# A two-layer attention and expert block: router logits and token rows made block by block from x before its norm

## The chip, the cores and the metric

One Trainium2 chip, one core of it. The metric is the device time of one execution in microseconds (us); the figure is the median over runs. TensorE's clock has two levels, 1.2 and 2.4 GHz, and the profile shows the granted share of the higher one for each stretch.

## The reference

256 latent tokens and 256 context tokens of width 1024 go through two layers. Only what comes before and around the router matters here:

```python
x_lat = x_lat + g1 * y_lat                                   # y_lat = merged branches @ w_out
h_lat = rmsnorm(x_lat, norm2_g[l]) * (1.0 + sc2) + sh2
x_lat = x_lat + g2 * grouped_moe(h_lat, ...)                 # the context tokens too, in layer 0

def merge_branches(...):
    g = sigmoid(h @ w_gate + b_gate)
    m = g_a * (o_a @ w_br_mla) + g_b * (o_b @ w_br_na) + g_c * (o_c @ w_br_ft)
    return m @ w_out

def grouped_moe(h, router_w, router_bias, w_g, w_u, w_d):
    scores = sigmoid(h @ router_w)                           # 16 experts in 4 groups of 4
    sel = scores + router_bias
    grp_score = top_k(sel by group, 2)[0].sum(-1)            # the best group, then
    ...                                                      # the 2 best experts in it,
    top_w = top_w / sum(top_w)                               # weights from scores
    hid = silu(h @ w_g[e]) * (h @ w_u[e]) * gate
    return hid @ w_d[e]
```

## The kernel before

**Layout.** All activations are held by feature: `x` is 128 partitions x 8 blocks (kb) x 512 tokens in f32. Large products are made in three passes of 32-bit reduced matmuls (helper `three`, L1436 to L1440): each operand is split into a high part (a cast) and a low part (value minus high part). Weights come in chunks of 1 MB through a ring of five places (`raw`), in halves of 128 x 1024: ScalarE casts the high part (`half_high`, L518), VectorE subtracts to get the low part (`half_low`, L878). TensorE counts used halves in `w_used`, and the two engines run at most four halves ahead.

**Queues.** Each engine has one program, written out by hand, and takes its instructions in order. The waits are on semaphores: `full` and `free` of the 8 PSUM banks, and counters such as `hlo_done`, `mlo_done`, `perm_done`. VectorE's helper `link` waits for the instruction just issued. The function `results` hands out banks ahead of time, in turn or by name.

**Start.** ScalarE squares x block by block, VectorE adds the squares of blocks 0 to 5 (`gather_square`, L894), TensorE sums the result and the last two squares over the partitions (`norm_sum`, L1464, f32, two instructions for each matmul) and spreads the root (`norm_spread`, L1472). The modulation vector is made in four early pieces (`condition`, L1515, and `turn_rows`, L1523), woven between the blocks of the first latent projection (`latent`).

**Merge** (TensorE from L1746, ScalarE L764, VectorE L1162). Four groups of 256 columns. Each has three gate chunks and one branch chunk. The branch chunk has two halves; the first half makes the attention branch for both 128-column blocks (c = 0, 1), the second the other two branches. VectorE waits for the whole chunk, multiplies and adds (L1178 to L1182), ScalarE casts `m_hi` (L784), VectorE makes `m_lo` (L1186). In layer 0 all 512 tokens are carried (nq = 512), in layer 1 only 256.

**Out-projection** (TensorE L1763, VectorE L1190). Four groups (j) of two blocks, two halves each. VectorE adds the result onto x (L1203), ScalarE squares the blocks (L559).

**Second norm and router.** After the last group: `norm_sum`, root (L552), spread over a bank, then for each block VectorE scales x (L926), ScalarE adds the shift into `h_f` (L591), TensorE makes logits (L1795, 16 rows x nq, f32) and, by transposes (L1788), token rows. The sigmoid (L798) is turned again (L1805) to lie by token. VectorE ranks the experts by pairs in small linked instructions (`beaten`, L1226 with the helper `tt`). TensorE counts the tokens ahead of each in its group (L1816 to L1822), VectorE makes the slot of each token and the permutation `perm` (L1306). The token rows in high and low part (L602, L1326) are gathered into 4 units of 128 slots by matmuls (L1836), then gates (`gsl`, L1844) and slots by row (L1851) are made.

**Experts.** Four units and up to three extra units (1 in layer 1), each against four experts. Step i = 0 of the loop is the first expert's up-projection; ahead of step 1 the extra units are gathered (L1924) from the same token rows.

Of the kernel before, what the change touches and what calls it, by code (L numbers as in the profile page):

```python
# [6 lines left out]
F32 = mybir.dt.float32  # L7
F32R = mybir.dt.float32r
# [4 lines left out]
P = 128  # L13
# [45 lines left out]
def build(nc, wts, xin, vecs, rope, dft, biases, out):  # L59
    ctx = ExitStack()  # L60
    with ctx:
# [15 lines left out]
        h_f = nc.alloc_sbuf_tensor_at("h_f", [P, KB, T], F32, offset=h_at)  # L77
        hraw = nc.alloc_sbuf_tensor_at("hraw", [P, T // P, D], F32, offset=h_at + 4 * KB * T)
# [11 lines left out]
        eps = place("eps", [P, 1], F32)  # L90
# [5 lines left out]
        junk = place("junk", [P, 1], F32)  # L96
        smx = place("smx", [P, 4, 8], F32)
# [46 lines left out]
        rt = place("rt", [P, 24, 4, N_EXP], F32, R0)  # L144
        scT = place("scT", [P, T], F32, A0 + 76 * K1)
# [6 lines left out]
        slots = place("slots", [P, 7 * P], F32, A0 + 88 * K1)  # L152
        S0 = A0 + 88 * K1 + 3584
# [3 lines left out]
        gs4 = place("gs4", [P, 8, 4], F32, S0 + 320)  # L157
# [30 lines left out]
        cs_done = sem("cs_done")  # L188
        spread_done = sem("spread_done")
# [93 lines left out]
        for l in range(DEPTH):  # L283
# [24 lines left out]
            s["merge"] = [{"gate": results(6, chunk=True), "br": results(6, chunk=True)} for _ in range(N_MERGE)]  # L308
            s["out"] = [results(2, chunk=True) for _ in range(N_OUT)]
            s["norm2"] = results(2, chunk=True)  # L310
# [5 lines left out]
            s["logit"] = results(1, [0])  # L316
            s["tok"] = [results(1, [1 + i % 6])[0] for i in range(KB)]
            s["score"] = results(1, [7])
            s["rank"] = results(1, [0])
            s["gs"] = results(2 * KB)  # L320
            s["gsl"] = results(1)
            s["row"] = results(1)
# [3 lines left out]
            s["gx"] = [results(1, [6 + i % 2])[0] for i in range(2 * KB)]  # L326
# [58 lines left out]
        def raw_wait(p):  # L385

            return raw_full[ring_slot[p]], 16 * (ring_turn[p] + 1)

# [71 lines left out]
        def _(pool):  # L460
            nc.gpsimd.memset(ident[:], 0.0).then_inc(consts, 1)
            nc.gpsimd.memset(ones[:], 1.0).then_inc(consts, 1)
            nc.gpsimd.memset(eps[:], EPS).then_inc(consts, 1)
# [11 lines left out]
                           allow_small_or_imprecise_dtypes=True).then_inc(tables, 1)  # L475
            nc.gpsimd.iota(first_of[:], pattern=[[P, 4]], base=0, channel_multiplier=0,
# [5 lines left out]
            pool.wait_ge(tables, 6)  # L482
# [22 lines left out]
        def _(act):  # L505
# [30 lines left out]
            def root(res, n, width):  # L536
                b, was = res

                act.wait_ge(full[b], nth(b, was))
                ins = nc.scalar.activation(rinv[:, 0:n], bank[b][:, 0:n], ACT.Sqrt, bias=eps[:], scale=1.0 / width)  # L540
                ins.then_inc(free[b], 1)

                return ins

            def preload(func):

                nc.scalar.activation(junk[:], eps[:], func)

            def norm_root(res, nt):

                act.wait_ge(sum_done, n_norm[0])
                nc.scalar.activation(rs[:, 0:nt // P], bank[res[0][0]][:, 0:nt // P], ACT.Sqrt, bias=eps[:],  # L552
                                     scale=1.0 / D).then_inc(free[res[0][0]], 1)

            def block_square(kb, nt):

                if kb >= 2:
                    act.wait_ge(acc_done, 5 * n_norm[0] + max(kb - 2, 1))
# [17 lines left out]
            def copies(l, which, nt):  # L576
                n0 = (2 * l + which) * KB
                to = h_hi if which == 0 else h_f
                for kb in range(KB):
                    if (l, which) == (0, 0) and kb % 2 == 0:  # L580

                        if kb < 4:
                            half_high(kb // 2)
                        mod_rows(kb // 2)
                        if kb == 4:
                            half_high(2)
                            half_high(3)
                    act.wait_ge(hf_done, n0 + kb + 1)
                    for st in range(nt // S_LAT):
                        c = slice(st * S_LAT, (st + 1) * S_LAT)  # L590
                        ins = nc.scalar.activation(to[:, kb, c], tmp[:, kb % 2, c], ACT.Identity,  # L591
# [1474 lines left out]
```

## Time and profile before

| | us |
|---|---|
| median of 3 runs | 1409.07 |
| lowest, highest | 1408.21, 1409.91 |
| profiled execution | 1407.64 |
| its span | 1405.9 |

| engine | busy us | share | instructions |
|---|---|---|---|
| TensorE, matmuls (PE) | 1295.9 | 92% | 6790 |
| TensorE, weight loads (PEld) | 1012.4 | 72% | 6790 |
| VectorE (DVE) | 886.5 | 63% | 1466 |
| ScalarE (ACT) | 695.8 | 49% | 1064 |
| GpSimd (POOL) | 14.7 | 1% | 28 |

Busy shares are means over stages. A wait is attributed to the engine whose signal came last; matmuls overlap with their neighbours, so the step from one start to the next, not the duration of one, is its price in a dense stretch. The DMA queues move 269 MB, mostly weights, at a mean of 191 GB/s.

### The profile page before, as it was taken

To read this page: it belongs to the slowest core of one execution; us is meant where nothing else is said; L and a number is where in the kernel's file an instruction comes from. 1 tells how busy PE (TensorE), PEld (TensorE's weight loads), DVE (VectorE), ACT (ScalarE), POOL (GpSimd) and SP (SyncE) were. 2 spreads that over 40 slices of the span, in tenths; PEclk is the share of its full clock that TensorE was granted. 3 is DMA by queue.
4 is the path that set the end of the run, shared out by engine and by line. 5 is a ranking of instruction groups with operands and counts; after the bars stand their busy time and mean duration, and the time that the engine had idled before them with its cause. 6 is when DMAs were issued, how large, how long until landed. Compare 5 with 4: busy or idle time off the path is not lost.

```text
span 1405.9 us, 18189 instructions
## 1 busy us (share of the span) xinstructions
PE 1295.9 (92%) x6790; PEld 1012.4 (72%) x6790; DVE 886.5 (63%) x1466; ACT 695.8 (49%) x1064; POOL 14.7 (1%) x28
## 2 busy tenths in 40 slices
PE   5999898989999988799999998899989986999996
PEld 4786555558888865688888886785479974788885
DVE  3655534342444245669999887667645656699985
ACT  3433333342332225358887666444343544588863
POOL 0100000000000000000000000100000000000000
PEclk9999999999999998899999999899999997899997
DMA  7722676642233211059999786332025540699980
GB/s 283 294 91 90 240 300 242 254 164 90 90 102 109 90 60 60 3 221 368 368 367 348 286 315 238 122 110 72 1 73 185 179 140 25 229 370 365 372 309 31
DMA packets 38277, 269.00 MB, mean 191 GB/s; under 512 B 4208, under 2 KB 5360, under 8 KB 5936
## 3 DMA queue, kind: packets, MB, share of 16 engines
q1 hardware_dynamic: 37232, 263.39, 51.2%
q0 software_dynamic: 960, 4.46, 0.8%
q8 instruction: 56, 0.92, 0.3%
q14 instruction: 29, 0.24, 0.0%
HBM read 266.78 MB, written 1.05 MB: 191 GB/s over the span
## 4 chain that ended last, share of the span: by engine, by line
PE 83%; DVE 11%; ACT 3%; issue 2%; DMA 0%; DVEq 0%; SPq 0%; ACTq 0%; PEldq 0%
PE bank L1438 20%; PE bank L1439 20%; PE bank L1440 20%; PE bank L1723 4%; PE bank L1515 3%; DVE lo L878 3%; PE bank L1707 2%; PE bank L1836 2%; PE bank L1682 2%; PE bank L1688 1%; PE bank L1924 1%; ACT w_hi L518 1%; PE bank L1795 1%; PE bank L1523 1%; DVE rt L1226 1%
## 5 line engine op out<-in xcount | busy, mean ns | idle before, releaser
L878 DVE TENSOR_TENSOR lo<-raw,w_hi 128x1024 fp32r<-128x1024 f32 x400 | 485.8, 1233 | 198.6 <-ACT w_hi L518 190.9
L518 ACT CAST w_hi<-raw 128x1024 fp32r<-128x1024 f32 x400 | 416.4, 1051 | 227.7 <-PE bank L1440 221.4
L1438 PE MATMUL bank<-h_hi,w_hi 128*128 128x512 f32 (+1 forms) x512 | 178.9, 349 | 14.0 <-DVE h_lo L938 8.8
L1439 PE MATMUL bank<-h_lo,w_hi 128*128 128x512 f32 (+1 forms) x512 | 177.2, 346 | 0.0
L1440 PE MATMUL bank<-h_hi,lo 128*128 128x512 f32 (+1 forms) x512 | 176.8, 345 | 0.0
L1438 PE MATMUL bank<-w_hi,h_hi 128*128 128x512 f32 (+1 forms) x320 | 127.5, 399 | 0.0
L1439 PE MATMUL bank<-lo,h_hi 128*128 128x512 f32 (+1 forms) x320 | 124.5, 389 | 0.0
L1440 PE MATMUL bank<-w_hi,h_lo 128*128 128x512 f32 (+1 forms) x320 | 123.9, 387 | 0.0
L1438 PEld LDWEIGHTS bank<-h_hi,w_hi 128*128 128x128 f32 x512 | 98.1, 192 | 33.2 <-issue 14.2
L1440 PEld LDWEIGHTS bank<-h_hi,lo 128*128 128x128 f32 x512 | 98.1, 192 | 11.7
L1439 PEld LDWEIGHTS bank<-h_lo,w_hi 128*128 128x128 f32 x512 | 98.2, 192 | 11.2
L722 ACT ACTIVATE prob<-bank,smx 128x512 f32<-128x512 f32 (+1 forms) x72 | 44.3, 616 | 92.7 <-DVE smx L1101 88.7
L1438 PE MATMUL bank<-w_hi,hdT_hi 128*128 128x512 f32 x192 | 76.2, 397 | 3.5 <-DVE hdT_lo L1359 3.5
L1440 PE MATMUL bank<-w_hi,hdT_lo 128*128 128x512 f32 x192 | 76.0, 396 | 0.0
L1439 PE MATMUL bank<-lo,hdT_hi 128*128 128x512 f32 x192 | 75.9, 395 | 0.0
L1440 PEld LDWEIGHTS bank<-w_hi,h_lo 128*128 128x128 f32 x320 | 60.8, 190 | 13.0
L1438 PEld LDWEIGHTS bank<-w_hi,h_hi 128*128 128x128 f32 x320 | 60.7, 190 | 11.8
L1439 PEld LDWEIGHTS bank<-lo,h_hi 128*128 128x128 f32 x320 | 60.8, 190 | 11.1
L784 ACT CAST m_hi<-g 128x512 fp32r<-128x512 f32 (+1 forms) x16 | 8.2, 513 | 114.4 <-DVE g L1182 114.4
L1178 DVE TENSOR_TENSOR g<-g,bank 128x512 f32<-128x512 f32 (+1 forms) x48 | 26.5, 553 | 53.2 <-PE bank L1440 48.5
L1438 PE MATMUL bank<-m_hi,w_hi 128*128 128x512 f32 (+1 forms) x128 | 45.2, 353 | 11.2 <-DVE m_lo L1186 11.2
L1707 PE MATMUL bank<-ident,prob 128*128 128x128 f32 x240 | 35.6, 290 | 20.2 <-DVE prob L1110 20.2
(230 smaller groups left out, 2169.7 us busy)
## 6 DMA issues: line engine op xcount, KB each, us to landing
raw<-weights SPq DMA_DIRECT2D x248, 1024.0 KB, 5.0
x<-tokens SPq DMA_DIRECT2D x2, 1024.0 KB, 6.1
nab<-na_bias POOLq DMA_DIRECT2D x2, 1024.0 KB, 8.3
rp<-rope POOLq DMA_DIRECT2D x2, 512.0 KB, 5.4
ft<-dft POOLq DMA_DIRECT2D x2, 512.0 KB, 6.0
out<-x SPq DMA_DIRECT2D x4, 256.0 KB, 2.2
fd<-dft POOLq DMA_DIRECT2D x2, 128.0 KB, 6.4
vec<-vectors SPq DMA_DIRECT2D x1, 176.0 KB, 2.4
```

Of the source, the lines that this page charges most:

```text
L518: nc.scalar.copy(w_hi[:, g % N_HI, :], raw[:, ring_slot[c], o:o + HALF]).then_inc(hi_done, 1)
L722: nc.scalar.activation(prob[:, i % 2, qb, 0:nk * P], bank[b][:, 0:nk * P], ACT.Exp, bias=smx[:, i % 2, 2 + qb:3 + qb], scale=scale, accum_ ...
L878: nc.vector.tensor_tensor(lo[:, ring_slot[c], o:o + HALF], raw[:, ring_slot[c], o:o + HALF], w_hi[:, g % N_HI, :].bitcast(F32), ALU.subtra ...
L1178: link(nc.vector.tensor_tensor(g3[:, a, c, 0:nq], g3[:, a, c, 0:nq], bank[b][:, 0:nq], ALU.mult))
L1438: nc.tensor.matmul(o, l_hi, r_hi, start=start, stop=False)
L1439: nc.tensor.matmul(o, l_hi, r_lo, start=False, stop=False)
L1440: return nc.tensor.matmul(o, l_lo, r_hi, start=False, stop=stop)
L1515: ins = nc.tensor.matmul(o[32 * j:32 * j + 32, :], cs[:, kb, :], raw[:, ring_slot[p], kb * CW:(kb + 1) * CW], start=(a == 0), stop=(a == 1))
L1682: ins = nc.tensor.matmul(bank[b][:, 0:nk * P], q[:, h, t], k[:, h, k0:k0 + nk * P], start=True, stop=True)
L1707: ins = nc.tensor.transpose(bank[b][:, o:o + P], prob[:, i % 2, qb, kb * P:(kb + 1) * P], ident[:])
L1723: ins = nc.tensor.matmul(bank[b][r:r + 64, 0:S_LAT], vv[:, k0 // P + kb, h * w:(h + 1) * w], probT[:, i % 2, kb, :], start=(kb == 0), stop ...
L1836: ins = nc.tensor.matmul(bank[b][:], h[:, t, kb * P:(kb + 1) * P], perm[:, t, 0:4 * P], start=(t == 0), stop=(t == nt - 1))
```

## The change

It changes what stands between the merge and the experts, and some things around it.

- `h_f` and `hraw` give way to `xc` (x times the norm gain and 1 + scale, without the root) and `xtok` (the same by token). After each out group VectorE writes two blocks of `xc`; TensorE, in the middle of the next group, makes their part of the logits by token (4 or 2 f32 matmuls with `xc` as the weights) and turns them (`token_block`). Blocks 6 and 7 follow after the last group, their logits in one stream with the sum of squares (bank 7).
- The root is applied per token: to the logits on VectorE, to the token rows on ScalarE (`htok_hi`) and VectorE (`htok_lo`), now one instruction per 128 tokens.
- The shift enters the logits as a sum over all features of shift x router weight (`shw`, `shift`), and the gathered rows as one more matmul with four rows (`sh4`, `in_slot`); the four rows are the shift of each of the two streams in high and low part. `in_slot` comes from a matmul of `perm` with a stream indicator.
- The gather adds high and low part in one bank; VectorE then makes `h_lo` as bank minus `h_hi`.
- The ranking compares all pairs in one instruction; the order of work after `perm` is new, and gates and slots by row are made ahead of step 1.
- In the merge the order within the branch chunk on VectorE is new (attention products after its first half; c = 0 before c = 1), and ScalarE and VectorE prepare weight halves at other points.
- At the start the first sum takes only the gathered squares, and `condition(1)` stands ahead of `latent(0)`.

The diff, cut to the parts that the prediction speaks of:

```diff
@@ VectorE, merge
+                    dve.wait_ge(w_used, 2 * s + 1)
+                    gated(0, 0)
+                    gated(0, 1)
+                    half_low(2 * s + 4)
+                    b, was = M["br"][0][2]
+                    dve.wait_ge(full[b], nth(b, was))
+                    gated(1, 0)
+                    gated(2, 0)
+                    merged(0)
+                    chunk_done(s)
+                    gated(1, 1)
+                    gated(2, 1)
+                    merged(1)
+                    merged_low(0)
+                    merged_low(1)
+                    half_low(2 * s + 5)
+                    s += 1
+
+                link(nc.vector.tensor_copy(sh2[:, :, 0:2], mod[:, l, 24:32, :]))
+                nc.vector.tensor_tensor(sh2[:, :, 2:4], mod[:, l, 24:32, :], sh2[:, :, 0:2].bitcast(F32), ALU.subtract)\
+                  .then_inc(sh2_done, 1)
+                for st in range(2):
+                    link(nc.vector.tensor_tensor(
...
+                nc.vector.tensor_reduce(shift[:], shw[:].rearrange("p s k e -> p s e k"), AX, ALU.add).then_inc(shw_done, 1)
@@ TensorE, out-projection
+                def token_block(kb):
+
+                    b, was = L["tok"][kb]
+                    claim((b, was))
+                    if kb == 0:
+                        claim((bs, wass))
+                    pe.wait_ge(xc_done, KB * l + kb + 1)
+                    for t in range(nt):
+                        nc.tensor.matmul(bank[bs][:, 16 + t * N_EXP:16 + (t + 1) * N_EXP], xc[:, kb, t * P:(t + 1) * P],
+                                         vec[:, V_RW + kb * N_EXP:V_RW + (kb + 1) * N_EXP],
+                                         start=(kb == 0 and t == 0), stop=False, skip_group_check=True)
+                    for t in range(nt):
+                        ins = nc.tensor.transpose(bank[b][:, t * P:(t + 1) * P], xc[:, kb, t * P:(t + 1) * P], ident[:])
+                    ins.then_inc(full[b], 1)
...
+                        if a == 0 and j == 0:
+                            b, was = L["shift"]
+                            claim((b, was))
+                            pe.wait_ge(shw_done, l + 1)
...
+                        if a == 0 and j > 0:
+                            token_block(2 * j - 2)
+                            token_block(2 * j - 1)
+                            if j < 3:
+                                shift_rows(j - 1)
@@ VectorE, router
+                def beaten(o, v):
+
+                    vi = v.rearrange("p t (i o) -> p t i o", o=1).to_broadcast([P, nt, 4, 4])
+                    vj = v.rearrange("p t (o j) -> p t o j", o=1).to_broadcast([P, nt, 4, 4])
+                    nc.vector.tensor_tensor(wins[:, 0:nt, :, 0:4], vj, vi, ALU.is_gt)
+                    tt(wins[:, 0:nt, :, 4:8], vj, vi, ALU.is_equal)
+                    tt(wins[:, 0:nt, :, 4:8], wins[:, 0:nt, :, 4:8],
+                       lower_of[:].rearrange("p (o i) j -> p o i j", o=1).to_broadcast([P, nt, 4, 4]), ALU.mult)
+                    total(o, wins[:, 0:nt])
@@ TensorE, gather
+                for kb in range(6):
+                    gathered_high(kb)
+                for kb in range(3):
+                    gathered_low(kb)
+                gathered_high(6)
+                gathered_low(3)
+                gathered_high(7)
+                for kb in range(4, KB):
+                    gathered_low(kb)
@@ TensorE, start
-                pe.wait_ge(acc_done, 5 * n + 5)
-                for i, part in enumerate((rinv, sq[:, 0, :], sq[:, 1, :])):
+                pe.wait_ge(acc_done, acc_from(n + 1))
+                parts = (rinv,) if n == 0 else (rinv, sq[:, 0, :], sq[:, 1, :])
...
                 if l == 0:
+                    condition(1)
                     latent(0)
-                    condition(1)
+                    turn_rows(1)
                     latent(1)
-                    turn_rows(1)
                     condition(2)
```

## Rows read from the trace of the kernel before

**Rows 1.** The page: chain that ended last, shares by engine.

```profile
PE 83%; DVE 11%; ACT 3%; issue 2%; DMA 0%; DVEq 0%; SPq 0%; ACTq 0%; PEldq 0%
```

**Rows 2.** Windows by stage. Columns: window, length, busy (x) of five engines, clock, DMA share, GB/s.

```profile
497.60:537.60 40.00, 39.95 (x162) 32.09 (x163) 16.05 (x24) 12.55 (x16) 0.00 (x0) 0.94 0.23 79
...
537.60:593.50 55.90, 43.79 (x196) 29.78 (x195) 36.38 (x111) 25.35 (x49) 0.88 (x1) 0.79 0.06 19
...
1157.60:1192.20 34.60, 22.88 (x104) 16.05 (x102) 25.41 (x93) 17.55 (x41) 0.88 (x1) 0.75 0.09 31
```

**Rows 3.** Timeline of the start. Columns: start, length, engine, line, operation, count, [idle before].

```profile
12.15 1.84 PE L1464 MATMUL bank<-ones,rinv 128*128 128x1 f32 x8 [12.15 <-DVE rinv L894]
...
17.33 3.64 PE L1515 MATMUL bank<-raw,cs 128*32 128x256 f32 x32
...
26.53 0.80 PE L1438 MATMUL bank<-h_hi,w_hi 128*128 128x512 f32 x1 [3.70 <-DVE h_lo L938]
...
31.64 1.93 PE L1515 MATMUL bank<-raw,cs 128*32 128x256 f32 x32
...
40.68 0.50 PE L1438 MATMUL bank<-h_hi,w_hi 128*128 128x512 f32 x1 [1.49 <-DVE h_lo L938]
```

**Rows 4.** Timeline of TensorE behind the last merge group of layer 0.

```profile
497.65 0.80 PE L1438 MATMUL bank<-m_hi,w_hi 128*128 128x512 f32 x1 [5.45 <-DVE m_lo L1186]
```

**Rows 5.** Waits of TensorE from 1100 to 1160: total, times, longest.

```profile
PE bank L1438 <- DVE m_lo L1186: 5.8, 1, 5.8
```

**Rows 6.** Windows of TensorE alone. Columns: window, length, busy (x), clock, DMA share, GB/s.

```profile
500.00:502.00 2.00, 2.00 (x6) 0.50 0.00 0
...
504.00:506.00 2.00, 2.00 (x10) 1.00 0.45 78
...
589.50:593.50 4.00, 4.00 (x38) 1.00 0.00 0
...
598.60:613.00 14.40, 13.64 (x68) 1.00 0.32 127
...
1137.00:1140.00 3.00, 3.00 (x15) 0.50 0.03 5
...
1144.00:1157.00 13.00, 13.00 (x113) 1.00 0.54 191
...
1197.50:1208.00 10.50, 8.30 (x37) 0.71 0.43 172
...
1208.00:1212.00 4.00, 4.00 (x11) 0.50 0.00 0
```

**Rows 7.** Groups of VectorE by form: busy us, mean ns, idle before.

```profile
L878 DVE TENSOR_TENSOR lo<-raw,w_hi 128x1024 fp32r<-128x1024 f32 x400 | 485.8, 1233 | 198.6 <-ACT w_hi L518 190.9 <-PE bank L1472 3.4
...
L1178 DVE TENSOR_TENSOR g<-g,bank 128x512 f32<-128x512 f32 x24 | 16.5, 686 | 37.7 <-PE bank L1440 35.4
...
L1110 DVE TENSOR_SCALAR prob<-prob,smx 128x256 f32<-128x256 f32 x24 | 8.5, 353 | 0.8
```

**Rows 8.** Timeline behind the out-projection of layer 0.

```profile
537.63 0.95 PE L1464 MATMUL bank<-ones,rinv 128*128 128x1 f32 x8
...
539.52 3.35 PE L1464 MATMUL bank<-ones,sq 128*128 128x1 f32 x16 [0.94 <-ACT sq L559]
...
557.79 1.09 PE L1788 MATMUL bank<-ident,h_f 128*128 128x128 f32 x8
...
559.27 0.22 DVE L1230 COPY rt<-bank 128x64 f32<-128x64 f32 x1 [5.73 <-PE bank L1805]
...
572.03 10.25 PE L1836 MATMUL bank<-perm,htok_hi 128*128 128x512 f32 x32 [5.80 <-DVE perm L1306]
```

**Rows 9.** Timeline of layer 1: an out group, and the scores.

```profile
1140.85 17.29 SPq L435 DMA_DIRECT2D raw<-weights  x4
...
1143.14 0.87 DVE L1203 SCALAR_TENSOR_TENSOR x<-bank,mod,x 128x256 f32<-128x256 f32 x2
...
1170.50 0.19 DVE L1230 COPY rt<-bank 128x32 f32<-128x32 f32 x1 [3.33 <-PE bank L1805]
```

More of the change, by code:

```diff
@@ L156, in build @@
         gsl = place("gsl", [P, 7, 4], F32, S0 + 192)
-        gs4 = place("gs4", [P, 8, 4], F32, S0 + 320)
+        over = place("over", [P, 4, 3], F32, S0 + 320)
+        ahead = place("ahead", [P, 4], F32, S0 + 384)
+        past = place("past", [P, 4], F32, S0 + 416)
+        over4 = place("over4", [P, 4, 4, 3], F32, A0 + 82 * K1)
         gx9 = place("gx9", [P, 3, 3], F32, S0 + 448)
@@ L804, in _ @@
                     act.wait_ge(full[b], nth(b, was))
-                    nc.scalar.copy(h_hi[:, kb, :], bank[b][:]).then_inc(free[b], 1)
-                b, was = L["row"][0]
-                act.wait_ge(full[b], nth(b, was))
-                nc.scalar.copy(sbr[:, 0:nq], bank[b][:, 0:nq]).then_inc(free[b], 1)
+                    nc.scalar.copy(h_hi[:, kb, :], bank[b][:]).then_inc(gshi_done, 1)
                 n_it, n_ext = L["n_it"], L["n_ext"]
@@ L1209, in _ @@
+                    if j == 0:
+                        b, was = L["shift"]
+                        dve.wait_ge(full[b], nth(b, was))
+                        nc.vector.tensor_copy(shift[:], bank[b][:, 0:2 * N_EXP].rearrange("p (s e) -> p s e", e=N_EXP))\
+                          .then_inc(free[b], 1)
+                    s += 1
                 dve.sem_inc(x_done, 1)
-                low(s + 1)
-                norm(l, 1, nq)
-                nt = nq // P
+                nt, ns = nq // P, nq // S_LAT
@@ L1312, in _ @@
                   .then_inc(g4_done, 1)
+                gathered_low(5)
+                half_low(2 * s + 3)
                 for t in range(nt):
@@ L1464, in norm_sum @@
                         ins = nc.tensor.matmul(bank[b][:, t:t + 1], part[:, t * P:(t + 1) * P], ones[:, 0:1],
-                                               start=(i == 0 and t == 0), stop=(i == 2 and t == nt // P - 1))
+                                               start=(i == 0 and t == 0),
+                                               stop=(part is parts[-1] and t == nt // P - 1))
                 ins.then_inc(sum_done, 1)
@@ L1845, in _, with gather @@
                                                start=(t == 0), stop=(t == nt - 1))
-                ins.then_inc(full[b], 1)
-                b, was = L["row"][0]
-                claim((b, was))
-                pe.wait_ge(diag_done, l + 1)
-                for t in range(nt):
-                    ins = nc.tensor.matmul(bank[b][:, t * P:(t + 1) * P], ones[:], diag[:, t, :], start=True, stop=True)
-                ins.then_inc(full[b], 1)
+                    ins.then_inc(full[b], 1)
+                def gather(res, h, kb, c0, c1, start):
+                    b, was = res
+                    for t in range(nt):
+                        pe.wait_ge(htok_done if h is htok_hi else htlo_done, t0 + t + 1)
+                        nc.tensor.matmul(bank[b][:, 0:c1 - c0], h[:, t, kb * P:(kb + 1) * P], perm[:, t, c0:c1],
+                                         start=(start and t == 0), stop=False)
@@ new lines, in shifted, with gathered_high @@
+                def shifted(res, kb, c0, c1):
+                    b, was = res
+                    bi, wasi = L["ind"][c0 // 512]
+                    pe.wait_ge(free[bi], wasi + 1)
+                    for bh, wash in L["sh4"]:
+                        pe.wait_ge(free[bh], wash + 1)
+                    nc.tensor.matmul(bank[b][:, 0:c1 - c0], sh4[:, kb * P:(kb + 1) * P], in_slot[:, c0:c1],
+                                     start=False, stop=True).then_inc(full[b], 1)
+                def gathered_high(kb):
+                    claim(L["gs"][kb])
+                    gather(L["gs"][kb], htok_hi, kb, 0, 512, True)
```

512 lines of the change are left out of this document (292 added, 220 removed).

## The prediction, made before the change was run

> **What bounds the kernel now.** First the chain that ended last: TensorE has 83% of it and VectorE 11% [rows 1]. So time that leaves TensorE's own stream is gained, time added to it is lost, and beyond that only the stretches where TensorE waits for VectorE count. The windows by stage show where those are [rows 2]. In the out-projection of layer 0 TensorE is busy 39.95 of 40.0 us. Between the projection's end (537.6) and the first expert matmul (593.5) it is busy 43.8 of 55.9 us at a mean clock of 0.79, and the same stage of layer 1 has 22.9 of 34.6 us. VectorE works 36.4 us of that first stage, mostly in tiny linked instructions. Three more gaps are in the code the change touches: the first matmuls of the program, 3.70 and 1.49 us inside the first latent projection [rows 3], and the wait for m_lo after the last merge group, 5.45 us in layer 0 [rows 4] and 5.8 us in layer 1 [rows 5]. Each gap costs more than itself. After the 5.45 us the granted clock is 0.50, 1.2 GHz (6 matmuls in 2 us where 9 to 10 run at 1.00, the 2.4 GHz level: 0.43 us a step and, over long stretches, 0.233) [rows 6].
>
> I write T for the end of the last merge group and E for the end of the out-projection; the sum is made on the profiled execution.
>
> **Start.** The sum of squares goes from 24 instructions to 8, as VectorE adds two more squares first. Now it begins at 12.15 with 8 in 1.84, and the condition matmuls start at 17.33 [rows 3]. After: two adds of 0.69 [rows 7] bring the begin to 13.45, and 8 instructions end at 15.3, so 2.0 us earlier. Condition(1), 1.93 us [rows 3], moves from behind latent(0) into the 3.70 us wait: 1.9. Its rows are then turned earlier, so latent(2) no longer waits 1.49. Latent(0) ran its 12 matmuls at 0.43 us a step where 0.23 is the full-clock step, and with less idle time ahead of it should run fast: 2.0. Sum -7.4; bounds 0 (if the weight chunks land no earlier) and -8.
>
> **End of the merge.** The products of block c=0 are multiplied as soon as its banks are full, 2.8 us before T in layer 0. VectorE's chain then is: two products (0.69 each [rows 7]) and two adds to T+0.1, the same for c=1 to T+3.0, the two m_lo to T+4.4. TensorE has 30 matmuls, 7.0 us, of other work behind T before it wants block 6, so the 5.45 us wait goes, and with it the slow stretch of 4.5 us behind it, worth 2.3. But a new wait appears: after the first half of out group 0 TensorE needs the shift logits, and VectorE reaches them only behind a half_low (1.23 [rows 7]) and six small instructions (about 1.4): T+7.0, TensorE is there at T+5.6. Costs 1.4. Queued behind that wait is the whole rest of the projection. Layer 0: -5.45 - 2.3 + 1.4 = -6.3. In layer 1 a half is 2.8 us (24 steps of 0.115 [rows 6]) and VectorE's chain hardly shorter: products and adds 0.42 to 0.45 each (0.44 for 256 columns out of a bank [rows 9]), end of m_lo at T+4.0, half_low to T+5.25, shift at T+6.7, TensorE waiting from T+2.8. So 5.8 becomes 3.9, and the slow clock behind it (3 us at 0.50 [rows 6], worth 1.5) stays half of the time: -2.6.
>
> **Out-projection, which TensorE bounds.** It takes in six token blocks, two shift rows and the shift logits. A logit matmul in f32 is two instructions bound by the weight load, like the sum over squares: 8 in 0.95, so 0.119 [rows 8]. A turn is one of 0.128 (8 in 1.09 with its end) [rows 8]. Layer 0: 4 x 2 x 0.119 + 4 x 0.128 = 1.46 a block, six are 8.8. Eight turns of the shift in f32 at 0.24 are 1.9 (bounds 1.0 and 2.0), the logits 0.25. Sum +10.9. Layer 1 has two token tiles: six at 0.73 are 4.4, with 2.15 that is 6.5. There TensorE also waits: the x update starts 2.3 us after a group's end (group end 1140.85, 1143.14 [rows 9]), two of 0.44, then the scaled copy 0.35 [rows 7]: T'+3.6, while TensorE is through the next half at T'+2.8. Three times 0.8: +2.4. Sum +8.9. In layer 0 the same chain ends 5.2 us after the group, inside the next half of 5.6.
>
> **From E to the first expert matmul.** Layer 0 now: 8 and 16 sum instructions, the latter at 0.21 (slow clock); scores on VectorE at 559.27 = E+21.6; gather at 572.03 = E+34.4 [rows 8]; 64 matmuls in 17.5; then 28 + 8 instructions for gates and rows, 4.0 at full clock [rows 6]; expert at E+55.9. After, at the slow clock for this piece, since the same quiet work lowers it today: squares at E+1.75, 16 sums to E+5.2, 16 logit instructions to E+8.6; root, table load (1.3) and two token copies of 0.6 on ScalarE, sigmoid done at E+11.9. VectorE to the group mask: 9 linked instructions of 0.18 to 0.28, E+14.2. Counting matmuls, 16 at 0.21, with four VectorE instructions under them: E+17.7. Nine small instructions E+19.5, four perm of 0.62 to E+22.1, indicator products to E+23.9. The gather has 64 + 8 matmuls at 0.233, 16.8, plus 0.8 while the clock recovers: E+41.5. Gates and rows (4.0) are not gone, they stand in step 1 on TensorE now. So 41.5 against 55.9 - 4.0: -10.4. The token rows' low part (4 x 1.3) is done at E+27.3, before TensorE wants it at E+30. Layer 1 the same way: sums and logits to E+3.3, sigmoid E+6.1, mask E+8.2, counts E+10.1 (8 at 0.22), first perm E+12.5, indicator E+13.8, gather 40 x 0.233 = 9.3 + 2.4 slow: E+25.5. Today the scores start at 1170.50 [rows 9] = E+12.9, and the expert at E+34.6 [rows 2] of which 1.5 is gates and rows: 33.1. Gain -7.6.
>
> **The gather of the extra units, in step 1.** It now uses one bank per block in place of two. Layer 0: 14.4 us [rows 6] become 72 x 0.17 = 12.3 plus 0.3: -1.8. Layer 1: 10.5 us of which 2.2 idle, and 4 us at 0.50 behind it [rows 6]. After, two banks in turn, each 0.6 (TensorE) + 0.35 + 0.4, is 0.75 a block, 6; if the clock still falls 8.8. I take 7: -3.5.
>
> **Sum:** -7.4 - 6.3 - 2.6 + 10.9 + 8.9 - 10.4 - 7.6 - 1.8 - 3.5 = -19.8. The profiled execution takes 1407.64 us, 1.74 of it outside its span, and lies 1.43 below the median of the runs shown. So 1407.64 - 19.8 + 1.43 = 1389.3. The router's own rewrite is nearly even (10.9 + 8.9 against 10.4 + 7.6): its work leaves a stage where TensorE is partly idle for one where it is not. The gain is the start, the merge and step 1.
>
> **The rivals.**
> (A) Slower: the clock falls inside the out-projection. Token blocks and shift rows are up to 3.9 us of narrow matmuls between dense halves. Each fall would double that piece (about +3 in layer 0, +1.9 in layer 1) and run 4.5 us of the next half at 0.50 (+2.3, +1.6): six of them are 26 us, giving 1415. It decides from four falls of six (+17.6), where the kernel is about even. For it: the 8 narrow sum instructions at 537.63 with 1 us idle behind them are followed by 0.21 steps [rows 8]. Against it: 4.0 us of narrow work at 589.5 keep 1.00 [rows 6]. The Trainium skill (TensorE: Matmul & The Clock Gate, "A second HAM failure mode: psum-queue depth-cycling") tells of short idle moments between matmul groups that move the clock to and fro; by that rule this case would happen, and the 4.0 us row does not agree. Chance 0.08.
> (B) The start stays bound by the arrival of weights and by the modulation chain, and keeps only 2.0 of 7.4; VectorE, with shift, scaled copies and gather parts in its queue, adds 3 more: 1389.3 + 5.4 + 3 = 1398. For it: the matmuls are only one of three things the start needs, and each of the four modulation rounds passes through ScalarE and VectorE. Against it: latent(0) starts behind the very chain (sum, condition(0), spread) that gets shorter. Chance 0.22.
> (C) Quiet pieces behind E run at full clock: 48 + 16 instructions at 0.12 in place of 0.21 in layer 0 is -4.5, rank in layer 1 -0.9, and step 1 of layer 1 stays fast, -3: 1381. Layer 1 shows full clock behind E today, layer 0 doesn't. Chance 0.15.
> (D) Nothing measurable: the ranking chain doesn't shorten, for each paired instruction waits for its result just the same. My count has about 22 linked steps where there are 53; were it 40, 18 x 0.2 x 2 = 7 us come back: 1396, still faster; with B's 9 on top it is 1405, and that is within 0.2% of now (about what a measurement of this kernel can tell from no change). Chance of the two together 0.05.
> The forecast itself, 1384 to 1395, has 0.50. A to D and the forecast make 1.
>
> **Range and chances.** From (C) with 2 us to spare, 1379, to (B) with 3, 1401; outside are (A) and (D). Faster by over 0.2%: forecast, (B) and (C), 0.87; within: (D), 0.05; slower: (A), 0.08.
>
> **What would show it.** Right: no wait on m_lo at the merge's end; a wait of TensorE for VectorE's shift of 1 to 2 us in layer 0 and 3 to 4 in layer 1; the out-projection of layer 0 10 to 12 us longer at clock 1.00; first perm near E+20 and E+12.5; the first feature projection ending about 7 us earlier. Wrong: a clock of 0.5 between out groups, TensorE waiting for xc in layer 0, or a gather bound by VectorE's or ScalarE's copies out of the banks.

## The result, and the profile after

The changed kernel takes 1399.98 us (median, 1399.35 to 1400.46) where the kernel before takes 1408.71 (1408.21 to 1409.91) on the same chip: 0.9936 of it, 95% interval 0.9919 to 0.9954. Timed again beside the later experiments it was 1398.82, a ratio of 0.9928 (0.9913 to 0.9942). So it is faster, by 9 to 10 us; the forecast was 19.8. The two profiled spans are 1405.9 and 1397.9, 8.0 apart. Executions of one kernel differ with the granted clock (the kernel before on another chip: 1408 us at a mean clock of 0.958 to 0.960, 1412 to 1413 at 0.954 to 0.957), so each time below stands with its ratio to the kernel before on the same chip and the 95% interval of that ratio.

First the windows by stage of the changed kernel, cut at the events of the table below (columns as in [rows 2]): start, latents to their first square sums, attention (two), merge of layer 0, its out-projection, its end to the first expert matmul, steps 0 and 1 up to the second feature projection of step 1, experts, layer 1 up to its merge, and then the same stages of layer 1 (whose out-projection is cut here 0.5 us ahead of its first matmul, which starts at 1117.91).

```profile
0.00:24.37 24.37, 8.70 (x83) 5.42 (x83) 10.60 (x25) 11.64 (x20) 2.49 (x18) 1.00 0.94 376
24.37:59.50 35.13, 34.62 (x209) 27.02 (x210) 21.25 (x44) 15.92 (x27) 5.28 (x5) 1.00 0.79 316
...
300.15:478.20 178.05, 178.05 (x769) 146.03 (x770) 67.37 (x77) 51.54 (x63) 0.00 (x0) 0.99 0.25 89
478.20:534.83 56.63, 55.26 (x284) 45.13 (x282) 25.07 (x49) 19.48 (x26) 0.00 (x0) 1.00 0.22 75
534.83:577.52 42.69, 35.51 (x145) 25.85 (x143) 24.47 (x64) 15.90 (x24) 0.90 (x1) 0.76 0.07 25
577.52:602.90 25.38, 25.38 (x134) 20.85 (x133) 11.30 (x21) 8.91 (x14) 0.00 (x0) 1.00 0.23 84
...
1117.40:1154.71 37.31, 31.44 (x249) 29.56 (x247) 19.14 (x40) 15.68 (x26) 0.00 (x0) 0.95 0.32 114
1154.71:1182.25 27.54, 20.22 (x78) 13.16 (x76) 17.42 (x52) 12.63 (x22) 0.90 (x1) 0.75 0.11 38
1182.25:1199.77 17.52, 16.94 (x80) 14.20 (x79) 9.95 (x22) 7.19 (x14) 0.00 (x0) 0.80 0.33 121
```

The stages in both traces, each cut at the start of its first matmul, and what the prediction had for each (its steps regrouped to the cuts, us):

| stage | before | after | difference | forecast |
|---|---|---|---|---|
| start, to the first square sums of the latents | 67.34 | 59.46 | -7.9 | -7.4 |
| attention and merge, layer 0 | 417.71 | 418.73 | +1.0 | 0 |
| out-projection, layer 0, with the wait at its head | 52.58 | 56.64 | +4.1 | +4.6 |
| its end to the first expert matmul | 55.68 | 42.69 | -13.0 | -14.4 |
| steps 0 and 1 with the extra units' gather | 19.45 | 25.33 | +5.9 | +2.2 |
| other experts, layer 0 | 269.04 | 270.18 | +1.1 | 0 |
| layer 1 up to the end of its merge | 245.48 | 244.88 | -0.6 | 0 |
| out-projection, layer 1, with its waits | 30.34 | 36.80 | +6.5 | +6.3 |
| its end to the first expert matmul | 34.61 | 27.54 | -7.1 | -9.1 |
| steps 0 and 1, layer 1 | 15.03 | 17.52 | +2.5 | -2.0 |
| the rest | 198.64 | 198.13 | -0.5 | 0 |

The miss is 11.8 us, and 11.6 of it stand in the four rows behind the two projections, where the gathers are. Each of the other rows is within 1.1 us.

The waits of TensorE in the changed kernel's two out-projections (478 to 540 us, then 1117 to 1160; total, times, longest). The m_lo of [rows 4, 5] is gone; the shift logits have taken its place.

```profile
PE bank L1915 <- DVE shift L1266: 1.4, 1, 1.4
...
PE bank L1915 <- DVE shift L1266: 3.1, 1, 3.1
PE bank L1880 <- DVE xc L1289: 2.4, 3, 0.8
```

And the tail behind the projection of layer 0, where [rows 8] stood (timeline of TensorE; the last line is VectorE's):

```profile
534.83 0.95 PE L1930 MATMUL bank<-ones,rinv 128*128 128x1 f32 x8
536.62 2.85 PE L1930 MATMUL bank<-ones,sq 128*128 128x1 f32 x16 [0.84 <-ACT sq L591]
539.34 3.57 PE L1935 MATMUL bank<-vec,xc 128*128 128x16 f32 x16
...
548.16 0.58 PE L1951 MATMUL bank<-rt,before 128*128 128x16 f32 x2 [3.46 <-DVE rt L1355]
...
553.73 1.28 DVE L1385 TENSOR_SCALAR perm<-slots,slot 128x896 fp32r<-128x896 f32 x2
```

The first of the four perm instructions starts at E+18.9 (forecast E+19.5) and the last ends at E+21.4 (22.1). The first gather matmul starts at E+23.1 (23.9), in layer 1 at E+13.1 (13.8). So routing got ready a little earlier than forecast, and yet the first expert started 1.4 and 2.0 us later than forecast: the time went into the gathers, 19.6 us in place of 17.6 and 14.4 in place of 11.7.

### The profile page after: what moved, and what is told of

Its sections match the earlier page's. It is cut to its first block, busy times and chain, and to the rows that moved or that the text cites. A ratio compares the mean times of both kernels' runs of the same rounds, so it can differ in the third digit from the quotient of the medians.

```text
span 1397.9 us, 18387 instructions
## 1 busy us (share of the span) xinstructions
PE 1306.0 (93%) x6908; PEld 1024.3 (73%) x6908; DVE 877.4 (63%) x1426; ACT 693.1 (50%) x1038; POOL 15.0 (1%) x30
## 3 DMA queue, kind: packets, MB, share of 16 engines
HBM read 266.78 MB, written 1.05 MB: 192 GB/s over the span
## 4 chain that ended last, share of the span: by engine, by line
PE 87%; DVE 8%; ACT 2%; issue 2%; DMA 0%; DVEq 0%; SPq 0%; PEldq 0%; ACTq 0%
PE bank L1539 21%; PE bank L1541 20%; PE bank L1540 20%; PE bank L1826 4%; PE bank L1977 3%; PE bank L1618 3%; PE bank L1810 2%; PE bank L1785 2%; DVE lo L929 1%; PE bank L1791 1%; PE bank L1626 1%; PE bank L2066 1%; PE bank L2067 1%; DVE prob L1162 1%; PE bank L1987 1%
## 5 line engine op out<-in xcount | busy, mean ns | idle before, releaser
L1541 PEld LDWEIGHTS bank<-h_hi,lo 128*128 128x128 f32 x512 | 98.0, 191 | 11.8
L1540 PEld LDWEIGHTS bank<-h_lo,w_hi 128*128 128x128 f32 x512 | 98.2, 192 | 11.3
L1539 PE MATMUL bank<-w_hi,hx_hi 128*128 128x512 f32 x128 | 51.9, 406 | 0.0
L1618 PE MATMUL bank<-raw,cs 128*32 128x256 f32 x768 | 48.0, 392 | 3.0 <-PE bank L1826 3.0
L1541 PE MATMUL bank<-w_hi,hx_lo 128*128 128x512 f32 x128 | 50.7, 396 | 0.0
```

The source lines that it names most:

```text
L1539: nc.tensor.matmul(o, l_hi, r_hi, start=start, stop=False)
L1540: nc.tensor.matmul(o, l_hi, r_lo, start=False, stop=False)
L1541: return nc.tensor.matmul(o, l_lo, r_hi, start=False, stop=stop)
L1618: ins = nc.tensor.matmul(o[32 * j:32 * j + 32, :], cs[:, kb, :], raw[:, ring_slot[p], kb * CW:(kb + 1) * CW], start=(a == 0), stop=(a == 1))
```

## Experiments: the 4-row shift product

In the gather one line is new: `shifted`, which adds the shift of a token's stream to every slot by a product with four rows. A low block with it (four products, the shift product, and the start of the next block), then a block of step 1, in the changed kernel (timeline of TensorE):

```profile
564.83 1.19 PE L1977 MATMUL bank<-perm,htok_lo 128*128 128x512 f32 x4
565.95 0.50 PE L1987 MATMUL bank<-in_slot,sh 4*128 4x512 f32 x1
566.38 0.73 PE L1977 MATMUL bank<-perm,htok_lo 128*128 128x512 f32 x2
...
587.88 0.86 PE L1977 MATMUL bank<-perm,htok_lo 128*128 128x384 f32 x4
588.67 0.44 PE L1987 MATMUL bank<-in_slot,sh 4*128 4x384 f32 x1
589.04 0.98 PE L1977 MATMUL bank<-perm,htok_hi 128*128 128x384 f32 x4
```

From 564.83 to 566.38 are 1.55 us for five steps, where five of 0.233 are 1.17. And the weight load in this place waits, for nothing that the profile can name (timeline of the weight loads):

```profile
564.40 0.18 PEld L1987 LDWEIGHTS bank<-in_slot,sh 4*128 4x128 f32 x1 [0.35 <-issue]
564.83 0.30 PEld L1977 LDWEIGHTS bank<-perm,htok_lo 128*128 128x128 f32 x2 [0.25 <-issue]
```

Theory S: going from 128 rows to 4 and back keeps the loads from running under the matmul before. Rivals: the product costs its columns and the time is elsewhere (W); the three semaphore waits ahead of it cost the time (Q).

**no_shift_product.** The matmul of `shifted` is taken out.

```diff
-                    nc.tensor.matmul(bank[b][:, 0:c1 - c0], sh4[:, kb * P:(kb + 1) * P], in_slot[:, c0:c1],
-                                     start=False, stop=True).then_inc(full[b], 1)
```

> The changed kernel without the 32 products of sh4 and in_slot that add the shift to the gathered rows (the shift is left out of the experts' input). Theory S, the 4-row products are what was mis-sized: in the changed kernel's trace a low block with one takes 1.55 us and four plain steps are 0.93, so 0.62 x 8 in layer 0 and 0.62 x 8 in layer 1; in step 1 it is 1.97 against 1.56, 0.41 x 8, and some 0.35 x 8. Sum 16: about 1384 us. Rival W, each costs its columns as the prediction had it (0.233 and 0.17, narrower in layer 1), and the missing time lies in the clock or in copies out of the banks: 5.6, about 1394 us.

Measured: 1384.84 us, 0.9808 (0.978 to 0.9837), 15 to 18 less than the changed kernel: theory S, not W. (It leaves the shift out of the experts' input, so it only serves to time the rest.)

**waits_once.** The three `wait_ge` only `if kb == 0`.

> The changed kernel with the three semaphore waits ahead of each 4-row product (ind bank, sh4 bank twice) kept only ahead of the first block, where they are not yet met. Rival Q, the waits in TensorE's queue delay the product: up to 0.39 x 16 + 0.2 x 16 = 9 less, about 1391 us. Theory S, the load of 4 rows is what doesn't overlap: no change, 1400 us.

Measured: 1397.86 us, 0.9919 (0.9888 to 0.9949), and the gather's stretches (from the first gather matmul to the first matmul behind step 1's gather) are 45.6 and 32.0 us, where the changed kernel beside the later runs has 45.5 and 31.9. Q falls.

**shift_twice.** The matmul stands twice, the first with `stop=False`.

> The changed kernel with each 4-row product issued twice in a row into the same bank (the shift is added twice). If every 4-row product pays for its own load (0.18 + 0.23 and more): 32 x 0.4 to 0.5, about 1415 us. If only the change from 128 rows to 4 and back costs, the second costs its columns: 5.6 more, about 1406 us.

Measured: 1414.73 us, 1.0015 (0.9994 to 1.0036), which agrees with the first number. But the ten executions run from 1407.2 to 1417.0 us, four of them below 1411 at a mean clock of 0.962 to 0.964 and six above 1413 at 0.956 to 0.958, so the total can't decide between the two. The trace, of an execution of 1409.28 us, can (timeline of TensorE):

```profile
565.19 0.49 PE L1987 MATMUL bank<-in_slot,sh 4*128 4x512 f32 x1
565.53 0.39 PE L1989 MATMUL bank<-in_slot,sh 4*128 4x512 f32 x1
565.85 1.19 PE L1977 MATMUL bank<-perm,htok_lo 128*128 128x512 f32 x4
566.97 0.49 PE L1987 MATMUL bank<-in_slot,sh 4*128 4x512 f32 x1
```

A low block's period goes from 1.55 to 1.78 us (+0.23), one of step 1 from 1.97 to 2.15 (+0.18): the second product costs its columns. The stretches grow by 4.2 and 4.1 us. So the change of shape is paid once for each visit. The span is 10.4 us above that of the changed kernel; some 2 us of it are not located.

**rows_128.** `sh4` and `in_slot` get 128 rows, 124 of them zero; `wide_of` stands in for `of_stream`.

```diff
-        sh4 = place("sh4", [4, D], F32R, A0 + 74 * K1)
+        sh4 = place("sh4", [P, D], F32R, A0 + 74 * K1)
+        wide_of = place("wide_of", [P, 2, P], F32R, A0 + 80 * K1)
...
-        in_slot = place("in_slot", [4, 7 * P], F32R, A0 + 88 * K1)
+        in_slot = place("in_slot", [P, 7 * P], F32R, A0 + 88 * K1)
```

> The changed kernel with sh4 and in_slot of 128 rows, 124 of them zeros (one more ScalarE instruction and three VectorE ones in the out-projection), so that the shift product has the shape of the others. Theory S: a step as any other, so 16 - 5.6 = 10 us less than the changed kernel, about 1390 us, and no idle weight load ahead of the line. Rival: it is not the row count but the end of the accumulation or the waits: 1400 us.

Measured: 1388.17 us, 0.9839 (0.9811 to 0.9866), 11 to 13 us less than the changed kernel, with nothing left out. Spans 1386.6 against 1397.2, 10.6 apart. Its timeline of TensorE:

```profile
562.67 1.07 PE L1988 MATMUL bank<-perm,htok_lo 128*128 128x512 f32 x4
563.58 0.39 PE L1998 MATMUL bank<-in_slot,sh 128*128 128x512 f32 x1
563.80 1.07 PE L1988 MATMUL bank<-perm,htok_lo 128*128 128x512 f32 x4
```

A block is 1.13 us, the stretches are 38.8 and 27.3 us: 11.3 less, while no_shift_product has 37.8 and 26.6. Two products of the same content, with 4 rows or with 128, differ by 0.42 us a block.

**rows_64 and rows_32.** rows_128, but the product reads `sh4[0:64, ...]` and `in_slot[0:64, ...]` (or `0:32`).

> rows_128 with the shift product reading only rows 0 to 63 of the padded tiles (the writes stay those of rows_128). If the load waits whenever the number of rows changes between neighbours: a low block of 1.55 us as with 4 rows, gather's stretches 45.2 and 31.6 us, some 1399 us. If only a few rows are the trouble: 1.13 us a block, 1388 us as rows_128.

> The same with rows 0 to 31. Change of row count: as with 4 rows, 1399 us. Few rows only: between rows_64 and the 4-row kernel. If the padded writes and not the shape of the product were what helped in rows_128, both would be at 1388 us with blocks of 1.13 us.

Measured: 1397.66 us, 0.9926 (0.9899 to 0.9953), and 1399.42 us, 0.9935 (0.9915 to 0.9955). Stretches 45.2 and 32.0, 45.5 and 31.9 us, as with 4 rows. With 64 rows:

```profile
562.74 0.50 PE L1998 MATMUL bank<-in_slot,sh 64*128 64x512 f32 x1
563.16 1.18 PE L1988 MATMUL bank<-perm,htok_lo 128*128 128x512 f32 x4
564.27 0.50 PE L1998 MATMUL bank<-in_slot,sh 64*128 64x512 f32 x1
```

A period of 1.53. Whether it is 4, 32 or 64 rows hardly matters (1.55, 1.55, 1.53), nor do the padding's writes, which these kernels have too; that the number differs from its neighbours' does.

## Experiments: start, merge and the shift logits

**start_alone.** The kernel before with only the start of the change.

```diff
-            for kb in range(1, KB - 2):
+            for kb in range(1, KB):
                 gather_square(0, kb, T)
...
-                    latent(0)
                     condition(1)
+                    latent(0)
+                    turn_rows(1)
                     latent(1)
-                    turn_rows(1)
```

> The kernel before with the start of the change alone: the sum over squares from 24 instructions to 8 and condition(1) ahead of latent(0). The two traces put the start at -7.8 (first square sums of the latents at 67.3 against 59.5), the prediction at -7.4: about 1401 us, 0.9947. Rival: the start gains only because other parts of the change also moved, and the weights' arrival bounds it: -2, 1406.7 us.

Measured: 1402.65 us, 0.9955 (0.9939 to 0.9971): -6.3 (-4.1 to -8.6), the start's own. The stage varies between executions: its end stands at 62.4 us in this trace, at 59.5 and 60.9 in the two of the changed kernel, at 67.3 and 68.4 in two traces that have the old start (before and merge_alone).

**merge_alone.** The kernel before with the changed merge loops (`gated`, `merged`, `merged_low`, the bank marked full after block c=0).

> The kernel before with the early products of the merge alone, no shift logits behind it. The prediction's terms without the new shift waits: layer 0 -5.45 - 2.3, layer 1 -5.8 + 0.7 for the m_lo still late and -0.8 for the clock: -13, about 1395.5 us. Rival: the clock behind the merge falls anyway and the wait moves to the next bank: -7 or less, 1402 us or more.

Measured: 1391.46 us, 0.9873 (0.9857 to 0.9888): -17.9, more than expected. No wait of TensorE for m_lo is left in either layer; the first wait behind the merge of layer 0 is the one for ScalarE's square at the end of the projection:

```profile
PE bank L1484 <- ACT sq L563: 0.9, 1, 0.9
```

Layer 0's projection with the wait at its head falls from 52.6 to 44.8 us, 7.8 less (7.75 forecast without the shift); layer 1's from 30.3 to 22.9, 7.5 less where 5.9 were expected, since its wait goes whole. The spans are 16.2 apart.

**shift_early.** VectorE's five shift instructions stand ahead of the merge loop.

```diff
+                link(nc.vector.tensor_copy(sh2[:, :, 0:2], mod[:, l, 24:32, :]))
...
                 s = s0 + N_IN + N_UP
                 for j in range(N_MERGE):
...
-                link(nc.vector.tensor_copy(sh2[:, :, 0:2], mod[:, l, 24:32, :]))
```

> The changed kernel with VectorE's five shift instructions moved from behind the last merge group to ahead of the first one. Theory: the waits of 1.37 us (layer 0) and 3.15 us (layer 1) were VectorE's queue alone; layer 1 keeps about 0.7 for m_lo, so -3.9 and some clock: 1396 us. Rival: m_lo and the halves behind it are as late, so the wait only changes its name: 1399 to 1400 us.

Measured: 1392.51 us, 0.9887 (0.9872 to 0.9903), 5.8 to 6.3 less than the changed kernel beside it. TensorE has no wait for m_lo, the shift or a weight half in either projection; the three for xc in layer 1 stay. Windows of 31 us in layer 1's projection, both from 0.7 to 0.8 us behind its first matmul: first shift_early's, which ends with the projection, then the changed kernel's from its second profile, where 5 us of the projection still follow:

```profile
1116.00:1147.00 31.00, 28.61 (x242) 27.04 (x241) 16.86 (x32) 15.70 (x26) 0.00 (x0) 1.00 0.38 136
```

```profile
1118.00:1149.00 31.00, 26.25 (x206) 24.66 (x204) 16.21 (x32) 13.29 (x21) 0.00 (x0) 0.94 0.33 113
```

Over the whole projection the clock is 1.00 (31.9 us) and not 0.95 (36.8 us), so the wait had also lowered it. The changed kernel in these comparisons is after_again:

> The changed kernel as it is, beside the others on this chip: 1400 us as before, 0.993 to 0.994 of the kernel before.

Measured: 1398.82 us, 0.9928 (0.9913 to 0.9942), as expected.

## Experiments: what was moved, and the clock

**blocks_behind.** All token blocks of the out-projection stand behind it.

```diff
-                        if a == 0 and j > 0:
-                            token_block(2 * j - 2)
-                            token_block(2 * j - 1)
...
+                for kb in range(KB - 2):
+                    token_block(kb)
```

> The changed kernel with the six token blocks of the out-projection (48 logit and 24 turning instructions in layer 0, half in layer 1) all issued behind its last group. If a block costs the same wherever it stands (8.8 us in layer 0, 4.4 in layer 1 at full clock): the idle 0.8 and 0.7 us behind the projection are filled and layer 1 loses its 2.4 us of waits for xc, so -3.9, about 1395 us. Rival: behind the projection they run at half clock and hold up the root and the ranking, +4 to +10, 1403 us or more; then standing inside the projection was what the change gained by.

Measured: 1411.19 us (1402.96 to 1418.97), 1.001 (0.9982 to 1.0039): some 10 to 12 more than the changed kernel. The rival is confirmed. Six of the twelve executions lie within its size (1403.0 to 1408.1 us, mean clock 0.958 to 0.960), six above it (1414.2 to 1419.0, 0.949 to 0.952); the profile is of one of 1408.14. Timeline of TensorE behind the projection:

```profile
530.18 0.96 PE L1879 MATMUL bank<-vec,xc 128*128 128x16 f32 x8
530.99 0.63 PE L1883 MATMUL bank<-ident,xc 128*128 128x128 f32 x4
...
537.89 1.73 PE L1879 MATMUL bank<-vec,xc 128*128 128x16 f32 x8
539.46 1.09 PE L1883 MATMUL bank<-ident,xc 128*128 128x128 f32 x4
```

The same block is 1.28 us at first (530.18 to 531.46) and 2.46 later (537.89 to 540.35): the clock drops from 2.4 to 1.2 GHz while they run. Six blocks take 12.6 us here; between dense halves they run at clock 1.00 throughout.

**gates_first.** The row and gate products go back ahead of step 0.

```diff
+                b, was = L["row"][0]
+                claim((b, was))
...
                 for i in range(n_it + 1):
                     if i == 1:
-                        b, was = L["row"][0]
-                        claim((b, was))
```

> The changed kernel with the gate and row products (3.9 us in layer 0, 1.9 in layer 1) ahead of step 0 of the experts, as in the kernel before, and not in step 1. The prediction says that moving them is neither gain nor loss, since TensorE bounds both places: 1399 us, within 1.5. Rival: in step 1 they cover the time in which step 0's results are made, so undoing it costs up to 4 us, 1403.

Measured: 1419.49 us (1403.71 to 1425.55), 1.0034 (1.0002 to 1.0066): by the ratios some 14 to 15 us more than the changed kernel, over the rival's 4. This is a mean over two cases: four of the twelve executions took 1403.7 to 1409.1 us at a mean clock of 0.961 to 0.965, 5 to 10 more, and eight took 1418.6 to 1425.6 at 0.949 to 0.954. The profiled execution is one of the eight, of 1424.76. Step 1's gather in it (timeline, and the window over its blocks):

```profile
593.27 0.96 PE L1977 MATMUL bank<-perm,htok_hi 128*128 128x384 f32 x4 [1.89 <-ACT sbr L888]
594.07 1.40 PE L1977 MATMUL bank<-perm,htok_lo 128*128 128x384 f32 x4
595.40 0.68 PE L1987 MATMUL bank<-in_slot,sh 4*128 4x384 f32 x1
596.02 1.65 PE L1977 MATMUL bank<-perm,htok_hi 128*128 128x384 f32 x4
```

```profile
594.00:619.70 25.70, 25.70 (x69) 19.89 (x67) 4.35 (x8) 3.35 (x7) 0.00 (x0) 0.50 0.06 26
```

Without the gate products TensorE stands 1.89 us for ScalarE's copy of the row bank, which is queued behind a silu and a weight cast of 1.04 us. The first products of the gather still run at full clock; from 594 us on all of it runs at 0.50, 3.47 us a block where the changed kernel has 1.97. The 3.9 us of gates and rows cover that wait. That the four shorter executions had the wait and kept the clock is likely and not shown: none of them has a profile.

**rows128_early, best_a, best_b.** The repairs together. best_a adds the shift of layer 1 as a bias in the copies and moves token blocks behind the second half of an out group; best_b moves them in layer 1 only.

```diff
-                    nc.scalar.copy(h_hi[:, kb, :], bank[b][:]).then_inc(gshi_done, 1)
+                    if l == 0:
+                        nc.scalar.copy(h_hi[:, kb, :], bank[b][:]).then_inc(gshi_done, 1)
+                    else:
+                        nc.scalar.activation(h_hi[:, kb, :], bank[b][:], ACT.Identity, bias=mod[:, l, 24 + kb, 0:1])\
+                          .then_inc(gshi_done, 1)
...
-                        if a == 0 and j > 0:
+                        if a == (0 if l == 0 else 1) and j > 0:
```

> The changed kernel with both repairs: sh4 and in_slot with 128 rows, and the shift instructions ahead of the merge. The one gave 10 us in the gather's stretches, the other 5.8: if they add up, 1399 - 16 to 19, about 1382 us. Rival: they share the slow clock of layer 1, so that together they give 12: 1387 us.

> rows128_early, and three more: in layer 1, where all tokens have one shift, it is added as a bias in the copies out of the banks, with no shift rows, indicator or shift products; and in both layers the token blocks stand behind the second half of an out group, not behind the first. The waits for xc (3 x 0.8) and the idle 0.8 and 0.7 us behind the projection go, and some 2 us of TensorE's work in layer 1: 1382 - 2.4 - 1.5 - 2 = 1376 us. Rival: the bias copies are slower than plain ones and become the bound of layer 1's gather: 1381 us.

> best_a with layer 0's token blocks back behind the first half of an out group (layer 1's stay behind the second). In best_a, as in blocks_behind, the pair behind the projection runs at a clock of 0.5 and its tail takes 23.6 us where rows128_early has 21.8; taken back, layer 0 loses 1.8 us: 1374.4 us. Rival: the clock of the tail has nothing to do with the pair, then 1377 us or more, as the 0.8 us of idle time is back.

Measured: 1382.43 us, 0.9821 (0.9793 to 0.9848); 1376.19 us, 0.9761 (0.9741 to 0.978); 1374.40 us, 0.9756 (0.9729 to 0.9784). All three as expected, with layer 0's tail (first sum to first gather matmul) at 21.8, 23.6 and 21.6 us. That best_b beats best_a is not shown: the intervals of the ratios overlap, best_b's own executions run from 1370.6 to 1379.9 us, and the tail differs as much between two traces of the changed kernel (23.1 and 20.9). Both beat the kernel before by over 2% and the changed kernel by some 23 to 24 us.

## Why the prediction was wrong where it was wrong

The direction and the range held; the gain was 9 to 10 us in place of 19.8. The time came out at rival (B)'s number and not by its mechanism. By the prediction's own steps:

- **Start, right.** -7.4 forecast, -7.9 in the trace (-6.5 in the second one), -6.3 alone. Latent(0) starts at 24.37 with 0.23 us steps, 2.2 earlier, and latent(2) doesn't wait. Rival (B)'s -2.0 falls.
- **End of the merge, mechanism right, layer 1's size off.** The shift wait was 1.37 us (forecast 1.4) and 3.15 in layer 1 (3.9). The prediction named the shift as what TensorE would wait for, but booked it as what is left of the old wait ("5.8 becomes 3.9") and took its place in VectorE's queue as given. merge_alone shows that nothing of the old wait is left, and shift_early that the place of the shift was all of the new one. So the step earns 17.9 us alone, of which the change gives 5.8 to 6.3 back by five instructions in the wrong place.
- **Out-projection, right.** The differences of +4.1 and +6.5 us are within 0.5 of the forecast; clock 1.00 in layer 0, no wait for xc there, and three of 0.8 us in layer 1. Rival (A) did not happen, and blocks_behind shows the reverse: between dense halves is where this narrow work runs at full clock. The Trainium skill tells of short idle moments between matmul groups that move the clock to and fro (TensorE: Matmul & The Clock Gate, "A second HAM failure mode: psum-queue depth-cycling"); this case's trace doesn't show that between out groups, where shift_early's layer 1 keeps 1.00 through three waits of 0.8 us. The row of 4.0 us that the prediction set against it has no idle moment in it, so it didn't bear on that rule.
- **From E to the gather, right.** The first gather matmul came 0.8 and 0.7 us earlier than forecast; (D) falls. (C) happened in part at most: 16 logit instructions took 3.57 us in the first trace, 0.22 each, but 2.30 in the second trace of the same kernel. (C)'s own sum has a slip too: 64 instructions at 0.12 in place of 0.21 are 5.8 us, not 4.5.
- **The gather, the step that failed.** "The gather has 64 + 8 matmuls at 0.233", "72 x 0.17" and their likes for layer 1 priced each shift product as one more step. It costs 0.42 us more in layer 0's blocks, and some 0.35 on average over all 32: the stretches of rows_128 are 11.3 us shorter than after_again's and 10.8 shorter than those of the first trace. That is the miss of 11.8. With the shape repaired, three of the four gathers come out at the forecast or below: 16.8 us (17.6), 12.6 (12.6) and 11.5 (11.7), where the changed kernel has 19.6, 15.8 and 14.4. The fourth, step 1 of layer 1, takes 10.1 us, and 8.5 repaired, where the prediction took 7: its clock fell, and the prediction had 8.8 for that case. The time of the repaired kernel is 1388.2 us, the forecast was 1389.3; that they agree so closely is partly luck, as small misses of both signs cancel.
- **A row that would have warned.** The prediction took the step of a uniform series, with no bound above. The profile of before has products of 64 rows between products of 128, in attention (timeline of TensorE):

```profile
237.82 1.12 PE L1688 MATMUL bank<-nak,naq 64*128 64x512 f32 x2
238.87 0.70 PE L1693 MATMUL bank<-nab,ident_na 128*128 128x256 f32 x2
239.50 1.12 PE L1688 MATMUL bank<-nak,naq 64*128 64x512 f32 x2
```

  One round takes 1.68 us, 1.05 for the two of 64 rows and 512 columns and 0.63 for the two of 128 rows and 256 columns. Series of such products with 128 rows throughout (L1682) take 0.91 and 0.48 for two: 0.29 us more for there and back. None of the prediction's signs of being wrong looked at this term.
- **"The router's own rewrite is nearly even", wrong.** If the parts add up, all but the start and the merge's early products is -10.1 (after_again) less -6.3 and -17.9: +14, where the forecast, split the same way, has about +1. Of the 14, 11 is the shape of the shift product and about 6 the shift's place. What is left would be a gain of 3 us, which is within the joint uncertainty of these differences (each has 2 us and more), so it is not shown to gain.
- **Gates and rows moved at no gain, wrong.** They cover a wait of 1.9 us, and, in the execution that was profiled, with it the clock of the 15.8 us behind it, which became 27.1. The prediction named TensorE's work that moves but not what it would hide.

Of the mechanism behind the 0.42 us the runs show what sets it (a neighbour of another row count, once for each visit). The Trainium skill says of the array's modes that "Changing tiling mode (not just tile) drains the TensorE" (TensorEngine Tiling (Array Packing), "Key Properties"). It doesn't say that a product of fewer rows is such a change of mode; if it is read so, 32, 64 and 4 rows cost alike, twice in a row costs once, and 128 rows nothing, and all four runs agree. No run here shows the array's mode itself. The Trainium skill also says that a single product of 32 rows takes the time of one of 128 (TensorE: Matmul & The Clock Gate, "Why this matters for your kernels"); between products of 128 rows that doesn't hold here, a block takes 1.55 us in rows_32 and 1.13 in rows_128.

Left open: some 2 us of shift_twice's span, and what decides from one execution to the next whether the clock falls in gates_first and blocks_behind. The +1.0 us in attention and merge of layer 0 is not the change's: the same stage takes 417.7 us in the kernel before and in after_again.

## What to carry to other kernels

Price a matmul by its neighbours too: one with fewer rows between full ones pays for the change of shape, and here padding it with zero rows was cheaper. Before moving small instructions, write down what is queued behind them on their engine and what idle time they cover where they are; here five VectorE instructions cost 6 us by their place, and 3.9 us of TensorE's work earned 5 to 10 us by its in some executions and 20 to 27 in the others. Look at more than one execution before a few us are put down to the clock. Keep narrow TensorE work between dense work, not after it.

## What the runs showed of the hardware

At 512 columns and full clock, a product of 4, 32 or 64 rows between products of 128 takes 0.40 to 0.42 us more than one padded to 128 (period of a block 1.55, 1.55, 1.53 against 1.13 us); a second one right behind it costs 0.23. Its weight load shows 0.35 us of idle time that no semaphore explains, and the next load 0.25; in rows_128 both are gone. The clock can stay low under unbroken work: in the profiled execution of gates_first, 0.7 us behind an idle time of 1.89 us, it fell, and the gather's products ran at 0.50 for 25.7 us while TensorE was busy all the time. How the clock goes differs between executions of one kernel: the same 16 narrow sum and 16 logit instructions behind the projection took 6.1 us in one trace of the changed kernel and 4.0 in the other.
